# A two-layer encoder trunk: rows of the layer norm read and centred a pair ahead, rotations placed among the low parts

## What is computed

```python
def hybrid_layer(x, w_in, a_group_w, a_scale, b_sinks, c_rel_bias, w_out, ln_gain, ln_bias):
    h = jnp.einsum('bsd,de->bse', x, w_in)
    a_v, a_gate, b_q, b_k, b_v, b_gate, c_q, c_k, c_v, c_gate = jnp.split(h, _split_points(), axis=-1)
    a_out = pool_mixer(a_v, a_group_w, a_scale) * jax.nn.silu(a_gate)
    b_out = swa_sink_attention(b_q, b_k, b_v, b_sinks) * jax.nn.silu(b_gate)
    c_out = chunk_relbias_attention(c_q, c_k, c_v, c_rel_bias) * jax.nn.silu(c_gate)
    mix = jnp.concatenate([a_out, b_out, c_out], axis=-1)
    y = jnp.einsum('bse,ed->bsd', mix, w_out)
    return _layer_norm(DEEPNORM_ALPHA * x + y, ln_gain, ln_bias)

def rope_partial(x, pos):       # the first 16 of 64 dims of each head of B
    ...
    rot = jnp.concatenate([x1 * cos - x2 * sin, x2 * cos + x1 * sin], axis=-1)

def _layer_norm(x, g, b):
    mu, var = mean(x), mean((x - mu) ** 2)
    return (x - mu) * lax.rsqrt(var + LN_EPS) * g + b

def reference(x, ...):
    for l in range(DEPTH):      # DEPTH = 2
        x = hybrid_layer(x, w_in[l], ...)
    return x
```

## Time and profile before

| what | value |
| --- | --- |
| median of 3 runs | 2816.25 us (2815.71 to 2819.7) |
| the profiled execution's own time | 2820.24 us |
| its span, from first to last instruction | 2818.4 us |
| mean granted clock of TensorE | 0.997 |
| TensorE busy (matmul) | 2783.0 us, 99% |
| VectorE busy | 1827.0 us, 65% |
| ScalarE, GpSimd busy | 1271.7 and 1278.3 us, 45% each |
| DMA | 152 GB/s mean over the span |

### The profile page before, as it was taken

The page is one execution under the profiler, slowest core; times in us unless marked ns, Lnnn a source line. Parts: engine busy times, 40 slices in busy tenths (PEclk is TensorE's granted clock), DMA queues, the critical chain, the costliest instruction groups (busy, mean ns, idle before and its releaser), DMA issues.

```text
span 2818.4 us, 41183 instructions
## 1 busy us (share of the span) xinstructions
PE 2783.0 (99%) x12996; PEld 2322.1 (82%) x12996; DVE 1827.0 (65%) x2950; ACT 1271.7 (45%) x2628; POOL 1278.3 (45%) x927
## 2 busy tenths in 40 slices
PE   9999999999999999999999999999999999999998
PEld 7888888888888888888887878888888788788886
DVE  5666679623777777862267777896146778778625
ACT  4444466523444445652244445654234444456521
POOL 4444444444344434444444444444444444344441
PEclk9999999999999999999999999999999999999999
DMA  6555432355566533235577775334466777532442
GB/s 213 166 166 160 133 89 82 113 174 182 170 175 174 167 92 101 86 94 178 172 208 200 206 204 148 87 86 124 161 213 198 202 206 215 143 97 83 137 157 102
DMA packets 418502, 427.09 MB, mean 152 GB/s; under 512 B 215424, under 2 KB 256416, under 8 KB 414624
## 3 DMA queue, kind: packets, MB, share of 16 engines
q1 hardware_dynamic: 414544, 409.22, 49.4%
q10 hardware_dynamic: 3792, 15.73, 1.4%
HBM read 348.21 MB, written 79.78 MB: 152 GB/s over the span
## 4 chain that ended last, share of the span: by engine, by line
PE 88%; DVE 6%; DMA 3%; issue 1%; SPq 1%; ACT 1%; POOL 0%; DVEq 0%; ACTq 0%; POOLq 0%
PE acc L725 60%; PE sc L725 18%; PE pv L725 9%; DMA pt_raw<-c_prob_scratch 2%; PE sc L813 1%; DMA raw<-in_wall 1%; DVE mixl L1715 1%; DMA c_prob_scratch<-prob 1%; PE sc L769 1%; DVE res L1882 1%; DVE res L1891 1%; DVE mixh L1715 1%; DVE res L1894 1%; DVE pt L1715 0%; SPq L503 0%
## 5 line engine op out<-in xcount | busy, mean ns | idle before, releaser
L1682 POOL TENSOR_TENSOR wl<-raw,wh 128x512 fp32r<-128x512 f32 x920 | 1277.5, 1392 | 1496.8 <-ACT wh L1151 1486.7
L1151 ACT ACTIVATE wh<-raw 128x512 fp32r<-128x512 f32 x920 | 574.8, 630 | 1089.4 <-PE acc L725 747.5
L725 PE MATMUL acc<-xh,wh 128*128 128x512 f32 x2560 | 1007.7, 394 | 6.8 <-DVE mixl L1715 3.1
L725 PE MATMUL acc<-xh,wl 128*128 128x512 f32 x2560 | 998.3, 390 | 0.0
L725 PE MATMUL acc<-xl,wh 128*128 128x512 f32 x2560 | 998.2, 390 | 0.0
L725 PEld LDWEIGHTS acc<-xh,wh 128*128 128x128 f32 x2560 | 481.7, 188 | 103.7 <-DVE mixl L1715 4.4
L725 PEld LDWEIGHTS acc<-xh,wl 128*128 128x128 f32 x2560 | 480.9, 188 | 103.3
L725 PEld LDWEIGHTS acc<-xl,wh 128*128 128x128 f32 x2560 | 482.0, 188 | 92.3
L1715 DVE TENSOR_TENSOR xl<-prob,xh 128x512 f32 x48 | 55.9, 1165 | 237.3 <-ACT xh L1151 237.3
L725 PE MATMUL sc<-wh,mixh 128*128 128x512 f32 x496 | 193.5, 390 | 0.1
L725 PE MATMUL sc<-wl,mixh 128*128 128x512 f32 x496 | 193.0, 389 | 0.0
(11 more groups left out here) (233 smaller groups left out, 3724.4 us busy)
## 6 DMA issues: line engine op xcount, KB each, us to landing
raw<-in_wall SPq DMA_DIRECT2D x920, 256.0 KB, 2.7
res_scratch<-res ACTq DMA_DIRECT2D x12, 1024.0 KB, 4.2
res<-res_scratch SPq DMA_DIRECT2D x12, 1024.0 KB, 5.2
c_prob_scratch<-prob SPq DMA_DIRECT2D x64, 160.0 KB, 3.0
pt_raw<-c_prob_scratch SPq DMA_DIRECT2D x16, 640.0 KB, 5.0
res<-in_x SPq DMA_DIRECT2D x8, 1024.0 KB, 6.6
x_scratch<-res SPq DMA_DIRECT2D x8, 1024.0 KB, 5.2
x_t_scratch<-turned SPq DMA_DIRECT2D x128, 64.0 KB, 2.6
```

The lines of the kernel that those rows point to most:

```text
L725: return nc.tensor.matmul(o, lhsT, rhs, start=start, stop=stop)
L1151: return nc.scalar.activation(o, i, ACT.Copy, scale=scale)
L1682: nc.gpsimd.tensor_tensor(wl[:, s, :], raw[:, s, :], wh[:, s, :].bitcast(F32), ALU.subtract).then_inc(w_lo, 1)
```

## The change

Four things, in the third and fourth step and in the last sections:

- SP issues `load_ln` of pairs 1 to 3 at unit 1 of the pair instead of unit 8, without the wait for a used weight unit. Gain and bias stay at unit 13. Pair 0 and the second step stay.
- VectorE centres the slab of pair p + 1 at the end of pair p, once the slab alone is in (`ln_in` + 16); `gain` now waits for gain and bias. Pair 0 is centred in its own place. The second step keeps its order.
- In the last sections of the first, third and fourth step VectorE has rotations, low query and keys in other places among `c_lo`, `c_add` of C's last pair; in the fourth step ScalarE makes the high query and the high keys one or two weight splits earlier.
- The product of C's last pair (`c_tail_product`), its high part on ScalarE (`mix_hi`, now behind two more splits) and its low part come behind the turned values.

```diff
--- before.py
+++ after.py
@@ SP, pair_events @@
-                    if s == 8 and it:
+                    if it and s == (1 if p and not on_tensor(it) else 8):
 
-                        sp.wait_ge(w_used, unit(it, p * U_C) + (1 + RING))
+                        if s == 8:
+                            sp.wait_ge(w_used, unit(it, p * U_C) + (1 + RING))
                         load_ln(it - 1, p)
@@ ScalarE, last section of the fourth step @@
                     c_hi(it, last, 2)
+                    query_hi()
                     split(it, KV0 + 7, 3)
-                    query_hi()
                     split(it, KV0 + 8, 0)
                     c_low_rows(it, last, 2)
                     split(it, KV0 + 9, 1)
+                    b_keys_hi()
                     split(it, KV0 + 10, 2)
                     c_hi(it, last, 3)
                     split(it, KV0 + 11, 3)
-                    b_keys_hi()
...
-                    mix_hi(nb + 2 * C_PAIRS, last + MIX_C)
...
                 split(it, B0 + 6, 2)
                 split(it, B0 + 7, 3)
+                if not on_tensor(it):
+                    mix_hi(nb + 2 * C_PAIRS, last + MIX_C)
@@ VectorE @@
             def centre(it, n):
-                dv.wait_ge(ln_in, n * 48 + (192 * it + 48))
+                dv.wait_ge(ln_in, n * 48 + (192 * it + (16 if n and not on_tensor(it + 1) else 48)))
...
-            def gain():
+            def gain(it, n):
+                dv.wait_ge(ln_in, n * 48 + (192 * it + 48))
                 V_(V.tensor_tensor(res[:], res[:], per_column(0), ALU.mult))
@@ first_half @@
-                    if it:
+                    if it and p == 0:
                         centre(it - 1, p)
...
                     gate_ready(p * 2 + ((2 * C_PAIRS + B_TILES) * it + 2), 1)
+                    if it and p + 1 < C_PAIRS:
+                        centre(it - 1, p + 1)
@@ second_half @@
-                    centre(it - 1, p)
+                    if p == 0:
+                        centre(it - 1, p)
...
                     mix_lo(p * 2 + (nb + 1), p + MIX_A)
                     c_normalise(it, p, 2)
+                    if p + 1 < C_PAIRS:
+                        centre(it - 1, p + 1)
@@ last section @@
                     c_normalise(it, p, 3)
-                    c_lo(it, p, 2)
-                    c_add(it, p, 1)
                 elif not half(it):
...
+                def rotated_keys():
+                    if half(it):
+                        dv.wait_ge(hist_mv, layer(it) + 1)
+                    dv.wait_ge(qh_ok, ROTS * it + 2)
+                    keys_lo([k[:, HD:] for k in bkl], s0[:, 0:HALF], [k[:, HD:] for k in bk]).then_inc(bq_ok, 1)
+
                 dv.wait_ge(rope_in, 32 * (it + 1))
                 rotate(it, 0, KV0 + 3, 0)
+                if on_tensor(it):
+                    rotated_query(ROTS * it + 1, 0)
+                    rotate(it, 1, KV0 + 7, 1, 1.0)
+                    rotated_keys()
+                elif half(it):
+                    c_lo(it, p, 2)
+                    c_add(it, p, 1)
+                    rotated_query(ROTS * it + 1, 0)
+                    rotate(it, 1, KV0 + 7, 1, 1.0)
+                    c_add(it, p, 2)
+                    rotated_keys()
+                    c_lo(it, p, 3)
+                else:
+                    rotated_query(ROTS * it + 1, 0)
+                    c_add(it, p, 2)
+                    c_lo(it, p, 3)
+                    rotate(it, 1, KV0 + 7, 1, 1.0)
+                    rotated_keys()
+                rotate(it, 2, B0 + 3, 1, source=q_bank)
                 if not on_tensor(it):
-                    c_add(it, p, 2)
-                rotated_query(ROTS * it + 1, 0)
-                if half(it) and not on_tensor(it):
-                    c_lo(it, p, 3)
-                rotate(it, 1, KV0 + 7, 1, 1.0)
-                if not half(it):
-                    c_lo(it, p, 3)
...
                     c_add(it, p, 3)
-                if not on_tensor(it):
-                    c_tail_product(p, C_PAIRS * (it + 1))
-                dv.wait_ge(prod_ok, MIXES * it + 2 * C_PAIRS + 2)
                 rotated_query(ROTS * it + 3, 1)
                 dv.wait_ge(w_used, unit(it, B0 + 7) + (1 + RING))
                 V.transpose(vals, v_bank).then_inc(vt_ok, 1)
                 if not on_tensor(it):
+                    c_tail_product(p, C_PAIRS * (it + 1))
+                    dv.wait_ge(prod_ok, MIXES * it + 2 * C_PAIRS + 2)
                     mix_lo(nb + 2 * C_PAIRS, p + MIX_C)
```

More of the change, by code:

```diff
@@ L2022, in first_half @@
                     if it:
-                        gain()
+                        gain(it - 1, p)
                     if p:
@@ L2168, in _ @@
-                rotated_query(ROTS * it + 1, 0)
-                if half(it) and not on_tensor(it):
-                    c_lo(it, p, 3)
-                rotate(it, 1, KV0 + 7, 1, 1.0)
-                if not half(it):
-                    c_lo(it, p, 3)
-                if half(it):
-                    dv.wait_ge(hist_mv, layer(it) + 1)
-                dv.wait_ge(qh_ok, ROTS * it + 2)
-                keys_lo([k[:, HD:] for k in bkl], s0[:, 0:HALF], [k[:, HD:] for k in bk]).then_inc(bq_ok, 1)
@@ L2178, in _ @@
-                if half(it) and not on_tensor(it):
-                    rotate(it, 2, B0 + 3, 1, source=q_bank)
-                    c_add(it, p, 3)
-                elif not half(it):
-                    c_add(it, p, 3)
-                    rotate(it, 2, B0 + 3, 1, source=q_bank)
-                else:
-                    rotate(it, 2, B0 + 3, 1, source=q_bank)
-                if not on_tensor(it):
-                    c_tail_product(p, C_PAIRS * (it + 1))
-                dv.wait_ge(prod_ok, MIXES * it + 2 * C_PAIRS + 2)
+                if on_tensor(it):
[16 more added lines that the diff above has]
+                    rotated_keys()
```

## The result

| | before | changed |
| --- | --- | --- |
| median of 8 runs each, side by side | 2819.48 us | 2828.25 us |
| lowest and highest of these | 2815.71 and 2820.34 | 2824.44 and 2835.25 |
| the profiled execution's own time, its span | 2820.24, 2818.4 us | 2833.76, 2832.0 us |
| mean granted clock of TensorE | 0.997 | 0.995 |

A forecast was written before the change was run, and what follows sets the result against it. TensorE, 99% busy, pauses for single VectorE instructions placed too late. Terms -4.2 - 5.0 - 5.2 + 2.6 + 0.5 = -11.3 us take the median from 2816.25 to 2805.0 us, range 2797 to 2814.

The forecast's parts named there:

- First step's last section, -4.2 us: First step's last section: the 2.70 us stop ahead of block 3's product goes; minus 4.2 us, 1.5 of it clock.
- Third step's, "nothing": Third step's last section: it has no stop, so the new order there changes nothing.
- Fourth step's last section, -5.0 us: Fourth step's last section: the 3.5 us wait for turned values goes, with 1.5 us at the lower clock; minus 5.0 us.
- TensorE's own product of block 3 as the last thing waited for: Fourth step's last section: with this waited for last, the last low query ends near 2447, 4 us early.
- Rival 3: Last sections: turned values or keys come last, both stops stay, 9.2 us are missing: 2814.2 us; 10%.
- Third step's pairs, -5.2 us: Third step, pairs 1 to 3: 7.0 us of stops go, new waits cost 1.8 us; minus 5.2 us.
- The 0.6 us of stop per pair: Third step's pairs: centring at the pair's end makes TensorE wait 0.6 us for block 1's low part, three times.
- I take 0.5 in all: The earlier slab load delays stores behind it: bounds 0 and 2.34 us a pair, taken as plus 0.5 us in all.
- Fourth step's pairs, +2.6: Fourth step, pairs 1 to 3: new gate waits cost 7.0 us, old 5.0 us of waits shrink to 0.6; plus 2.6 us.
- rival 1: Clock falls behind the three new waits of 2.3 us, costing 1.5 us each: 2809.5 us; 20%.
- Centring, 1.9 to 3.9 us: Cost of the slab's centring on VectorE: between 1.9 and 3.9 us; the short one plus GpSimd's running subtraction was taken.
- Rival 5: Load ahead of block 0's store makes TensorE stop before block 0's product in six pairs: slower, 2827.5 us; 5%.

The follow-up runs named there:

- small-load run: Changed pairs with the last sections of before, loading only 32 of 2048 slab columns in pairs 1 to 3, against the kernel before: ratio 1.0022.

## Why the prediction was wrong

Between the -11.3 us of the sum and the +13.6 us of the two profiled executions lie 24.9 us. The third step's pairs make 15.6 of them, the fourth step's last section 6.0 and its pairs 4.0.

**First step's last section, -4.2 us.** Mechanism right, size read off one execution. In every execution with the new order the stop is away, but it was 1.4 us in the mean and not 2.7, and of the six times that it came in the first step the lower clock followed three times (behind 2.70, 2.13 and 1.97 us, not behind 1.96). **Third step's, "nothing".** Wrong the same way: a mean of 1.4 us was there to win, in other executions than the profiled one.

**Fourth step's last section, -5.0 us.** The step that failed is "TensorE's own product of block 3 as the last thing waited for". I let TensorE's arrival there set the end of VectorE's chain, took block 3's low part as in time, and pointed to the third step; but there this low part stands ahead of the rotated keys, and in the fourth behind them, with its high part behind the high keys on ScalarE. I also priced the keys at 3.8 us; they took 5.87. The wait for the turned values did go, and 5.2 us with it; the new stop took 6.2. With block 3's parts moved ahead the section gave 5.2 us. Rival 3 named turned values or keys as last; it was a third one.

**Third step's pairs, -5.2 us; they came to +10.4.** This is the step that failed first of all. "All 7.0 us go" held. The 0.6 us of stop per pair rested on the gate's old time, ahead of which nothing was to be moved. With the load ahead of block 0's store it came 3.0 us late. "I take 0.5 in all" is thus the term that fell: the load cost 7.4 us by itself, and without its bytes the same pairs came to -3.4 us. My reason for 0.5 was that ScalarE's wait of 2.34 us had cost TensorE nothing; but there VectorE was idle for 7.15 us behind it, and here its chain had 1.8 us free. Even these 1.8 us were read at one pair's end. At the end of pair 2 of the same trace the fold took 1.59 us, and block 1's low part ended at 1636.25, right ahead of the product at 1636.39; nothing was free there. Then the clock fell behind each stop, 1.6 to 1.7 us more each time.

**Fourth step's pairs, +2.6; +6.6.** The gate wait was right to 0.1 us, three times. The forecast kept the full clock; rival 1 had it fall, at 1.5 us each, and it cost 1.6 and 1.7 us behind the first two and nothing behind the third. The rest is in the old waits: 2.0 us of them stayed where 0.6 had been kept.

**Centring, 1.9 to 3.9 us.** It took 2.2 to 2.9 us in its new place; 3.87 us was never paid at a pair's end. In the small-load run it took 2.24 us where a subtraction of GpSimd ran beside it for 0.6 us, and 2.89 where one ran for 1.4. The Trainium skill (GPSIMD Engine Reference, Specifications) says that VectorE and GpSimd contend for their shared SBUF interfaces; the trace agrees, and the size comes from these rows.

**Rival 5** gave the sign, and its time of 2827.5 us lies next to the measured 2828.25. That is luck: of its mechanism the first half held (load, then store, then ScalarE), the place hardly. Ahead of block 0's product TensorE lost only 0.5 to 0.6 us in each of the third step's pairs, and 2.7 us in all at block 2's scores; the most, 10 us, was at block 1's low part, and in three pairs, not six. The rest of the loss is rival 1's clock and the stop ahead of block 3's product, which no rival had. I gave 5% to a cost whose upper bound outweighed all gains together.

What is left open: why the stop ahead of block 3's product comes in some executions and not in others. Just ahead of the stop of 2.70 us a step of the rotation took 1.76 us and a fold 2.75; in the run with the load alone, without a stop, the same two took 0.69 and 0.58, and block 2's low part came 1.3 us sooner. What makes them long was not tried by itself, and neither was the slab's load on another engine's queue.

## What to carry to other kernels

A large load that is issued earlier can delay what stands behind it on its queue. Find the small store or load there whose landing an engine waits for, follow it to the engine that bounds the kernel, and price it by that chain's slack, not by how early the load itself is wanted. Put work into a stretch in which the engine is idle, not ahead of a thing that is waited for; and before a stop of 1 to 3 us becomes a term, look for it in a second execution.

## What was unexpected of the hardware

The length of a stop alone didn't tell whether the clock fell. Behind the gate's stop of 2.19 us it stood at 0.51, as shown above; behind the third pair's of 2.18 us it stayed at 1.00. The longer stop of 2.34 us in the run with the load behind the store (shown above, at 2331.79) kept it full:

```profile
2332.00:2334.00 2.00, 2.00 (x15) 1.84 (x15) 1.83 (x5) 0.26 (x1) 0.79 (x1) 1.00 0.87 202
2334.00:2338.00 4.00, 4.00 (x19) 3.34 (x18) 2.36 (x6) 3.75 (x8) 0.02 (x1) 1.00 0.86 258
```

In the run with the centring where VectorE is idle, TensorE's stops of 2.13 us (ahead of 325.45) and 3.50 us (ahead of 2456.98) stand the wrong way round:

```profile
325.40:327.40 2.00, 1.95 (x9) 1.98 (x10) 0.62 (x1) 1.95 (x4) 0.00 (x0) 0.52 0.04 8
2457.00:2459.00 2.00, 2.00 (x13) 1.82 (x14) 1.93 (x6) 1.71 (x4) 2.00 (x2) 1.00 0.30 80
```

So a bound between 1.43 and 2.70 us, as the prediction had it from the earlier trace rows, was not a rule.
